# Banded attention with scores two units ahead and keys behind the tile shared by two heads; expert slots by one-hot matmuls

## What is computed

```python
    qc = q.reshape(b, nc, CHUNK, A_KV_HEADS, grp, d)
    kb = window_chunks(k.reshape(b, nc, CHUNK, A_KV_HEADS, d), A_WINDOW_CHUNKS)
    vb = window_chunks(v.reshape(b, nc, CHUNK, A_KV_HEADS, d), A_WINDOW_CHUNKS)
    sc = jnp.einsum('bnqkgd,bnjkd->bnkgqj', qc, kb).astype(jnp.float32) * (d ** -0.5)
    ...
    m = jnp.maximum(jnp.max(sc, -1, keepdims=True), sink)
    e = jnp.exp(sc - m)
    p = e / (jnp.sum(e, -1, keepdims=True) + jnp.exp(sink - m))
    o = jnp.einsum('bnkgqj,bnjkd->bnqkgd', p.astype(v.dtype), vb)
```

```python
    wts = pg_sel[:, None] * topv / jnp.sum(topv, -1, keepdims=True)
    eid = (gsel[:, None] * EXPERTS_PER_GROUP + topi).reshape(-1)
    order = jnp.argsort(eid)
    tok = order // TOP_K
    sizes = jnp.bincount(eid, length=N_EXPERTS).astype(jnp.int32)
    xs = xt[tok]
```

## Time and profile before

| | us |
|---|---|
| median of 3 runs | 3147.25 (3137.70 to 3148.67) |
| the profiled execution: time | 3152.14 |
| its span in the trace | 3150.5 |
| window attention, SP's first DMA to the first instruction of the next phase | 1315.83 to 1564.99 |
| slots known (L1801 ends) to POOL's copy for the first gather (L1895) | 2060.81 to 2110.92 |
| granted TensorE clock over the whole span | 0.918 of 2.4 GHz |

### The profile page before, as it was taken

The page is one execution under the profiler, slowest core; times in us unless marked ns, Lnnn a source line. Parts: engine busy times, 40 slices in busy tenths (PEclk is TensorE's granted clock), DMA queues, the critical chain, the costliest instruction groups (busy, mean ns, idle before and its releaser), DMA issues. The chain is left out here.

```text
span 3150.5 us, 46329 instructions
## 1 busy us (share of the span) xinstructions
PE 2696.0 (86%) x14668; PEld 2320.1 (74%) x14669; DVE 1656.8 (53%) x3021; ACT 1120.7 (36%) x1872; POOL 894.5 (28%) x682
## 2 busy tenths in 40 slices
PE   1999994997979979699899999419999999999980
PEld 1888884886868868699778887308888888888870
DVE  5233332565656656355444453417677557557747
ACT  2111111343444434344311110205466446446633
POOL 2111110100001000023213223045455455445624
PEclk9999997998989989867699999859999999999995
DMA  4344446556393663345434432508788787778945
GB/s 154 131 141 149 142 131 189 157 167 199 122 241 125 183 179 126 112 121 135 120 114 135 144 120 87 210 22 284 243 292 313 229 264 259 249 229 303 353 106 227
DMA packets 274501, 567.43 MB, mean 180 GB/s; under 512 B 41072, under 2 KB 135536, under 8 KB 271344
## 3 DMA queue, kind: packets, MB, share of 16 engines
q1 hardware_dynamic: 182448, 429.98, 41.0%
q0 software_dynamic: 19776, 65.06, 8.3%
q10 hardware_dynamic: 72192, 71.31, 6.6%
HBM read 434.57 MB, written 131.69 MB: 180 GB/s over the span
## 5 line engine op out<-in xcount | busy, mean ns | idle before, releaser
L1870 DVE TENSOR_TENSOR e_wl<-rw_raw,e_wh 128x1024 fp32r<-128x1024 f32 (+1 forms) x288 | 422.9, 1513 | 25.8 <-ACT e_wh L2027 25.8
L2027 ACT ACTIVATE e_wh<-rw_raw 128x1024 fp32r<-128x1024 f32 (+1 forms) x384 | 377.7, 1053 | 4.1 <-PE e_py L1992 4.1
L1870 POOL TENSOR_TENSOR e_wl<-rw_raw,e_wh 128x1024 f32 (+1 forms) x96 | 273.6, 2864 | 75.2 <-ACT e_wh L2027 75.2
L301 PE MATMUL j_pg<-qkv_w_hi,j_xh 128*128 128x512 f32 (+1 forms) x640 | 242.6, 379 | 1.5 <-DVE j_xl L419 1.5
L303 PE MATMUL j_pg<-qkv_w_lo,j_xh 128*128 128x512 f32 (+1 forms) x640 | 237.4, 371 | 0.0
L302 PE MATMUL j_pg<-qkv_w_hi,j_xl 128*128 128x512 f32 (+1 forms) x640 | 236.6, 370 | 0.0
L991 POOL TENSOR_TENSOR b_o<-b_parts 128x128 f32<-128x128 f32 x64 | 31.0, 485 | 704.9 <-ACT b_parts L1108 704.9
L1978 PE MATMUL e_p_up<-e_wh,e_xh 128*128 128x256 f32 (+1 forms) x784 | 225.4, 288 | 0.0
L1980 PE MATMUL e_p_up<-e_wl,e_xh 128*128 128x256 f32 (+1 forms) x784 | 221.6, 283 | 0.0
L1979 PE MATMUL e_p_up<-e_wh,e_xl 128*128 128x256 f32 (+1 forms) x784 | 221.6, 283 | 0.0
L1042 PE MATMUL b_pg<-b_g_wh,b_g_xh 128*128 128x512 f32 x512 | 209.2, 409 | 4.4 <-DMA b_g_xl<-xt_lo 3.6
(11 more groups left out here) (315 smaller groups left out, 7243.2 us busy)
## 6 DMA issues: line engine op xcount, KB each, us to landing
rw_raw<-w_gate_up SPq DMA_DIRECT2D x256, 512.0 KB, 5.5
rw_raw<-w_down SPq DMA_DIRECT2D x128, 512.0 KB, 8.1
b_g_xh<-xt_hi SPq DMA_DIRECT2D x64, 512.0 KB, 3.7
b_g_xl<-xt_lo SPq DMA_DIRECT2D x64, 512.0 KB, 4.8
gates<-b_g_out ACTq DMA_DIRECT2D x64, 256.0 KB, 3.2
m_gt<-gates SPq DMA_DIRECT2D x16, 1024.0 KB, 8.4
qk_hi<-j_qkh ACTq DMA_DIRECT2D x16, 832.0 KB, 4.5
qk_lo<-j_qkl ACTq DMA_DIRECT2D x16, 832.0 KB, 6.9
```

The source lines that it names most:

```text
L301: nc.tensor.matmul(out, xh[:, u, ks], w_hi[:, k, cs], start=(k == 0), stop=False)
L1870: (nc.gpsimd if done is w_lo_pool else nc.vector).tensor_tensor(wl[:, slot(e, s), :], raw[:, s:s + 1, :], f(wh[:, slot(e, s), :]), ALU.sub ...
L2027: nc.scalar.activation(wh[:, slot(e, s), :], raw[:, s:s + 1, :], ACT.Copy).then_inc(w_hi, 1)
```

## The change

**Window attention.**
- Loops are written out: every step has its constants.
- PE at unit n now does: scores(n+2), turn(n), values(n-1).
- Scores: the mask matmul comes first. In the even heads of a pair the band is stored own keys first, so each of the k-hi and k-lo products is two matmuls, of 128 and of 64 columns; odd heads keep the keys behind first. So the 64 + 64 columns "behind" of two neighbouring heads lie side by side in `pr`.
- Turn: two transposes of 128 columns, each with the keys behind of two heads, and four for the own keys; `tp`, `tph`, `tpl` are 128 x 256 for the unit in place of 64 x 512.
- Values: `vz` holds v behind the tile twice, in rows 0 to 63 for the even head and in rows 64 to 127 for the odd one, with zeros elsewhere. Per pair of heads two matmuls of 256 columns (L677, L678) and four of 128 (L681, L682), all on 128 rows.
- SP loads v in six DMAs for a tile in place of four. ACT: exponentials of n+1, then the copies of n. DVE: denominator of n-1, maxima of n+1, low parts of n-1, scaling of n-2.

**Routing.** The table is not written to DRAM. The slot is split into tile and row. With `here` = (tile of the slot == tile number) and `rows` = (row of the slot == 0..127), 32 matmuls of 256 columns (16 tiles of tokens by 2 choices) sum up, for each slot: tile number of its token + 1, lane, weight hi and weight lo. DVE and ACT and POOL prepare the factors, DVE reads off `idx` and `weight`. The loads of x1 are issued ahead of the zero rows; the write to `slot_pair` and two copies of token numbers are gone.

**Experts.** The load, the transposes and the copies of the table are gone; the first gather stands ahead of the zeroing of `acc`'s spare rows.

```diff
-        vp = ph.sb("vp", [CHUNK, 2, A_KV, 2, HD], F32R)
+        vz = ph.sb("vz", [P, 2, A_KV, 2, 2, HD], F32R)
...
+            def load_v(t):
+                u = t % 2
+                if t >= 2:
+                    sp.wait_ge(pv, 2 * t - 2)
...
+                    for j in range(2):
+                        sp.dma_start(f(vz[j * CHUNK:(j + 1) * CHUNK, u, :, j, half, :]), rows).then_inc(v_loaded[u], 16)
+                    sp.dma_start(f(vc[:, u, :, half, :]), src[t, :, 0:A_K].rearrange("p (g d) -> p g d", g=A_KV)).then_inc(v_loaded[u], 16)
...
+            for t in range(NT):
+                if t + 2 < NT:
+                    load_qk(t + 2)
+                if t and t + 1 < NT:
+                    load_v(t + 1)
+                if t:
+                    store(t - 1)
...
+                if n >= 2:
+                    pe.wait_ge(exped, n - 1)
                 for j in range(GH):
...
+                    nc.tensor.matmul(score(g, j), mask[:, 0:P], mask[:, m0 + odd * P:m0 + odd * P + W], start=True, stop=False)
+                    if odd:
+                        nc.tensor.matmul(score(g, j), q, kh[:, u, g, :], start=False, stop=False)
+                        last = nc.tensor.matmul(score(g, j), q, kl[:, u, g, :], start=False, stop=True)
+                    else:
+                        for k in (kh, kl):
+                            nc.tensor.matmul(score(g, j)[:, 0:P], q, k[:, u, g, CHUNK:W], start=False, stop=False)
+                            nc.tensor.matmul(score(g, j)[:, P:W], q, k[:, u, g, 0:CHUNK], start=False, stop=(k is kl))
...
+                for j in range(PAIRS):
+                    nc.tensor.transpose(tp[:, j, :], pr[:, g, j, P:2 * P], ident[:])
+                for j in range(GH):
+                    last = nc.tensor.transpose(tc[:, j, :], here_of(g, j), ident[:])
...
+                for pair in range(PAIRS):
+                    both = po[g][:, 2 * pair:2 * pair + 2].rearrange("p h s d -> p (h s d)")
+                    nc.tensor.matmul(both, tph[:, g, pair, :], there, start=True, stop=False)
+                    nc.tensor.matmul(both, tpl[:, g, pair, :], there, start=False, stop=False)
+                    for j in (2 * pair, 2 * pair + 1):
+                        out = po[g][:, j].rearrange("p s d -> p (s d)")
+                        nc.tensor.matmul(out, tch[:, g, j, :], here, start=False, stop=False)
+                        last = nc.tensor.matmul(out, tcl[:, g, j, :], here, start=False, stop=bool(j % 2))
...
+            for n in range(UNITS):
+                if n + 2 < UNITS:
+                    scores_of(n + 2)
+                turn(n)
+                if n:
+                    values_of(n - 1)
...
-            for t in range(NT):
-                for c in range(2):
-                    pool.indirect_dma_start(out=slot_pair, out_offset=bass.IndirectOffsetOnAxis(ap=slots[:, c, t:t + 1], axis=0),
-                                            in_=pair[:, t, c, :], in_offset=None).then_inc(scattered, 16)
-            pool.wait_ge(scattered, 16 * 2 * NT)
+            pool.wait_ge(in_tile, 1)
+            for c in range(2):
+                nc.gpsimd.tensor_tensor(values[:, c, :, 0, :], here[:, c], tile_f[:].unsqueeze(2).to_broadcast([P, NT, SLOTS]),
+                                        ALU.mult).then_inc(tiled, 1)
...
+                for t in range(NT):
+                    last = nc.tensor.matmul(table, rows[:, c, t, :], values[:, c, t].rearrange("p v n -> p (v n)"),
+                                            start=(c == 0 and t == 0), stop=(c == 1 and t == NT - 1))
+            last.then_inc(inverted, 1)
...
+            for c in range(2):
+                nc.scalar.activation(values[:, c, :, 1, :], here[:, c], ACT.Copy, scale=lane[:]).then_inc(weighed, 1)
+                for t in range(NT):
+                    last = nc.scalar.activation(values[:, c, t, 3, :], here[:, c, t, :], ACT.Copy, scale=pair_lo[:, c, t:t + 1])
...
+            tt(here, count_f[:, 0:SLOTS].unsqueeze(1).unsqueeze(1).to_broadcast([P, 2, NT, SLOTS]), along(slot_tile[:], SLOTS),
+               ALU.is_equal).then_inc(in_tile, 1)
...
+            for c in range(2):
+                tt(rows[:, c], count_f[:].unsqueeze(1).to_broadcast([P, NT, P]), slot_row[:, c, :].unsqueeze(2).to_broadcast([P, NT, P]), ALU.is_equal)
+                tt(values[:, c, :, 2, :], here[:, c], f(pair_hi[:, c, :]).unsqueeze(2).to_broadcast([P, NT, SLOTS]), ALU.mult).then_inc(valued, 1)
```

More of the change, by code:

```diff
@@ L492, in window_attention_phase @@
     UNITS = A_KV * NT
+    PAIRS = GH // 2
+    M = W + P
     with Phase(nc, "a") as ph:
@@ L531, in _, with load_qk @@
             sp.dma_start(sink[:], sinks.rearrange("a (g h) -> a g h", g=A_KV).to_broadcast([P, A_KV, GH])).then_inc(sink_in, 16)
-            for u in range(2):
-                sp.sem_inc(stored[u], 16)
-            def load_qk(t, u):
-                cols = bass.ts(t, P)
-                first = isinstance(t, int) and t == 0
+            def load_qk(t):
+                u, cols = t % 2, slice(t * P, (t + 1) * P)
+                if t >= 2:
+                    sp.wait_ge(scores, 2 * t - 2)
                 for half, src in ((0, qk_hi), (1, qk_lo)):
@@ L573, in _ @@
-            load_v(1, 1)
-            sp.wait_ge(scores, 2)
-            load_qk(2, 0)
-            with sp.Fori(0, NT // 2 - 2) as i:
-                step(2 * i + 1, 1)
-                step(2 * i + 2, 0)
-            step(NT - 3, 1)
-            sp.wait_ge(pv, 2 * (NT - 2))
-            load_v(NT - 1, 1)
-            for t in range(NT - 3, NT):
-                store(t, t % 2)
+                            sp.dma_start(f(dst[rows, u]), k[:, :, t * P - CHUNK:(t + 1) * P]).then_inc(qk_loaded[u], 16)
@@ L1529, in _, with route_phase @@
             over_steps(dve, step)
-def route_phase(nc, ident, x1, w_group, b_group, w_router, b_router, bounds, slot_pair, x1_pad, raw, load_raw):
+def route_phase(nc, ident, x1, w_group, b_group, w_router, b_router, bounds, idx, weight, x1_pad, raw, load_raw):
     NL = NG + NE
@@ L1600, in _ @@
             sp.wait_ge(raw_in, 16 * raw.shape[1])
+            sp.wait_ge(zeroed, 16)
         @block.gpsimd
@@ L1945, in _ @@
             pe.sem_inc(down_done, 1)
-            pe.wait_ge(tab_in, 16)
-            for n in range(2):
-                last = nc.tensor.transpose(px[:, n * (MAXT + 1):(n + 1) * (MAXT + 1)], tab[:, :, n], ident[0:MAXT + 1, 0:MAXT + 1])
-            last.then_inc(tab_turned, 1)
             def turn_x(g, half):
```

316 lines of the change are left out of this document (164 added, 152 removed).

## The result

The changed kernel takes 3037.55 us (median of 4, 3036.12 to 3050.11) against 3147.96 us (median of 4, 3137.70 to 3148.67). The ratio is 0.9672, 95% interval 0.9650 to 0.9694: 110 us less, where 3041 was forecast. The profiled execution is the longest of the four, 3050.11 us with a span of 3048.4; it stands against 3152.14 and 3150.5 of before, 102.1 us in spans.

A forecast was written before the change was run, and what follows sets the result against it. Bound by PE at a lowered clock in the window attention, then by a POOL chain in the routing; 75 + 30 + 1.5 = 106.5 us less, from the median 3147.25 to 3041 us, range 3018 to 3080.

The forecast's parts named there:

- What bounds the kernel: Window attention: PE always busy at granted clock 0.69; behind the routing's slots: a 49 us chain on POOL.
- PE's work: Window attention: 34 matmuls and transposes per unit, 3.8 us at the high clock, 7.1 at the low.
- Which clock: Window attention: without stalls between values and scores the clock rises after a few units and stays, near 0.95.
- Rival D: Window attention: the clock never rises, 30 units at 7.1 us, no gain there, 3115 us in total; chance 0.12.
- The slow start: Window attention: three units at the low clock behind the first, 7.1 us each, 21.3 us together.
- What is late next: Window attention: SP's loads set the pace, 8.3 us per tile; 4.3 us per unit taken, PE and DMA near.
- 0.2 for waits: Window attention: us per unit added for waits to SP's 4.1, giving 4.3.
- bounds of 3.8 and 5.0: Window attention, us per unit: PE alone at the low end, a held-up load and lagging DMA at the high.
- Sum of the phase: Window attention: start, slow units, 27 units at 4.3 and tail end at 1489.5 against 1565.0, 75 us less.
- Routing: Slots to gather: a chain of 20.4 us in place of 50.1, so 30 us less (24 to 34).
- Start of the routing: Loads of x1 issued ahead of the zero rows end PE's wait earlier: 0 to 3 us, 1.5 taken.

The follow-up runs named there:

- light_transfers: Changed kernel with v in three loads per tile, POOL's weight loads cut to 4 KB behind the second tile, routing products on DVE: 3034.68 us in one execution.
- after_again: The changed kernel unchanged, measured again on the same chip as its variants: ratio 0.9685 to the kernel before.
- att_only: The kernel before with only the new window attention, routing and experts as before: 3078.45 us, ratio 0.9799.
- v_in_three: Changed kernel with v also written packed by the projection, so a tile's v comes in three loads, not six: ratio 0.9674 to the kernel before.
- two_more_issues: Changed kernel with two more 4-byte DMAs per tile in SP's queue among the loads of v: ratio 0.9698 to the kernel before.
- values_64_rows: Changed kernel with the products of the keys behind of every even head on 64 rows again: ratio 0.9682 to the kernel before.

## Why the prediction was right, and where it was not

The time was 3.5 us under the forecast. That it came so near is in part luck: some steps missed, and their errors cancel.

- **What bounds the kernel** held: PE with its lowered clock, then the chain on POOL.
- **PE's work** per unit held: 3.79 and 3.97 us in turn, 3.89 in the mean, for 3.8. The five score matmuls of an even head, two of them of 64 columns, take 0.52 us, some 0.1 each.
- **Which clock**: the outcome held, the reason only in part. The step put the falls down to the stalls of the values and to what stands between values and scores. The runs show that two stalling heads of four leave the clock at 1.00, that the new shapes in the old orders get 0.71, and that the turn's place with the orders around it is worth 14 to 26 us of the 70, which needs the orders of ACT and DVE as well; the step said nothing of those. It also expected the high clock to stay once it had come: it fell again behind three of PE's waits. Rival D had 0.12; its mechanism, clock 0.50 throughout, is what came of one wrong order, and not of the transposes: with six of them in every unit the clock stood at 1.00 for 85 us in light_transfers. So the rule of the Trainium skill ("TensorE: Matmul & The Clock Gate", Part 4) that transposes do not count did not decide here.
- **The slow start**: three units at 7.1 were taken, there were one of 7.20 and one of 5.68, so turn 4 came at 1360.1, 21.3 us behind the first turn in place of 25.9. In after_again and att_only no unit at the start was slow (15.2 us), so the term was right only in that there can be such units.
- **What is late next**: named rightly, SP first (8.35 us per tile for the 8.3 worked out), transfers and PE close behind, and PE's waits are ended by loads of q and k. The size was off: 4.78 us per unit between turns 4 and 28 in place of 4.3. That is 3.89 of work, 0.61 of waits (14.5 us in ten waits over 24 units) and 0.28 of low clock behind the longest of them. The term "0.2 for waits" missed that a wait of PE can cost twice, as the wait and as the fall of the clock behind it. The value lies inside its bounds of 3.8 and 5.0. The prediction expected no waits on PE in SP's queue; there were eight, 24 us in all.
- **Sum of the phase**: 0.3 us late at the first turn, 4.6 gained up to turn 4, 10.1 lost over the next 27 units and 0.6 in the tail make the 6.4 by which the next phase missed its 1489.5.
- **Routing**: 18.0 for 20.4. ACT was 9.8 for 9.5, but DVE, taken as 7.4 us, was 10.2 beside POOL and ended last, at 2005.4 against ACT's 2005.0; PE needed 2.8 behind it, not 3.7; the end of the phase took 1.0 us and not 3.
- **Start of the routing**: PE's first transposes stood 9.52 us behind the phase's first DMA before and 7.97 now, 1.55 as taken; 1.5 came back behind them (70.1 us from there to the slots against 68.7, the clock 0.80 against 0.85). Over all profiles the stretch from the merge's start to the slots is 494.5 us with the new routing (mean of ten, 493.1 to 496.4) and 497.2 with the old (mean of four, 495.8 to 498.1): 2.7 less, inside the 0 to 3 given.

The sum forecast was 106.5 against 102.1 in spans, while the medians moved by 110: the execution profiled after the change is the longest of its four, and its attention the longest of the three profiles. No step of the sum is sharper than the 10 us by which that phase moves by itself.

## What to carry to other kernels

Where a stretch is bound by PE at a low clock, look at what interrupts its matmuls, and then at the loop that a new order closes: the same PE order gave clock 0.50 or 0.71 depending on where DVE and ACT put the maxima and the copies. When an engine is sped up by a half, write down every other pace per tile beforehand (here 7.8, 8.05 and 8.35 us): relieving only the first of them buys what lies between it and the next, and what the relief costs elsewhere comes off (here some 10 us in the projection). One profile of each kernel is not enough for a term of 5 us when a phase moves by 10 between executions.

## What the runs showed of the hardware

- Behind a wait of PE for a load the clock fell in some cases and not in others. It fell behind waits of 2.31 and 2.83 us in the changed kernel, 1.66, 1.67 and 1.89 in after_again, 1.55 in v_in_three and 1.03 in att_only, 0.4 to 2.1 us after PE had resumed, and was low for 3 to 13 us. It stayed high behind 1.38 (changed kernel) and 1.74 (two_more_issues). Here is after_again behind its 1.66 us; the same L678 that takes 0.28 us at the high level takes 0.42:

```profile
1413.99 0.36 PE L643 MATMUL a_s<-a_mask 128*128 128x192 f32 x1 [1.66 <-DMA a_kl<-qk_lo]
...
1417.39 0.42 PE L678 MATMUL a_o<-a_vz,a_tpl 128*128 128x256 f32 x1
```

- At the high level a head with 64-row matmuls between 128-row ones takes 0.71 us for four matmuls, with 64 or with 128 columns (before and values_64_rows), and 0.50 without the changes (the odd head of values_64_rows).
- A load of 4 bytes holds SP for 0.45 us and one of 32 to 256 KB for mostly 0.60 to 0.67; single issues took up to 1.2 us more with no wait of the queue shown.
- DVE's comparison of 2048 elements took 2.28 us alone and 4.02 beside an elementwise product on POOL.
